# A feed-forward stage with Strassen-like weight blocks: one product moved, unit slots that may wrap, norm sums moved to VectorE, four down-projection chunks

## The reference

```python
x = x + jnp.einsum('btd,de->bte', mix, w_o[l])
h = rmsnorm(x, ln2[l])
gate, up = jnp.split(jnp.einsum('btd,df->btf', h, w_gu[l]), 2, axis=-1)
x = x + jnp.einsum('btf,fd->btd', jax.nn.silu(gate) * up, w_down[l])
```

## Time and profile before

| what | value |
|---|---|
| median of 3 runs (lowest to highest) | 1065.31 us (1064.7 to 1066.32) |
| the profiled execution: its own time, and its span | 1065.55 us, 1063.7 us |
| busy: PE (matmul), DVE, ACT, POOL | 97%, 64%, 47%, 32% |
| share of PE in the chain that ended last | 75% |
| mean granted TensorE clock | 0.995 |

### The profile page before, as it was taken

How to read it: one execution, slowest core, us unless ns; L and a number is a source line. 1 busy time by engine, 2 the same in 40 slices (tenths; PEclk the granted TensorE clock), 3 DMA queues, 4 the chain that set the end, 5 groups by cost and what they waited for, 6 DMA issues and landing times.

```text
span 1063.7 us, 15328 instructions
## 1 busy us (share of the span) xinstructions
PE 1026.7 (97%) x5694; PEld 851.0 (80%) x5694; DVE 682.8 (64%) x1267; ACT 503.3 (47%) x927; POOL 344.0 (32%) x405
## 2 busy tenths in 40 slices
PE   9999999999889999999998999999999999999997
PEld 7887877787679898888887877866787777788886
DVE  6865666477746667666676666799865766425544
ACT  6433566463434344434434645555754554423323
POOL 1354533343221010000100836533435756521101
PEclk9999999999899999999999999999999999999999
DMA  8312332222254454444433846311222333222312
GB/s 288 100 61 80 101 97 75 71 82 77 79 143 114 100 120 95 127 102 114 113 77 89 203 120 199 110 60 59 80 70 83 104 112 109 80 99 80 113 64 79
DMA packets 42681, 109.83 MB, mean 103 GB/s; under 512 B 5472, under 2 KB 8992, under 8 KB 42608
## 3 DMA queue, kind: packets, MB, share of 16 engines
q1 hardware_dynamic: 36720, 96.80, 28.5%
q0 software_dynamic: 5472, 11.54, 6.8%
q10 hardware_dynamic: 416, 0.52, 0.2%
HBM read 100.74 MB, written 4.74 MB: 99 GB/s over the span
## 4 chain that ended last, share of the span: by engine, by line
PE 75%; DVE 15%; ACT 5%; issue 4%; POOL 1%; DVEq 0%; ACTq 0%; POOLq 0%
PE bank L1739 16%; PE bank L1741 16%; PE bank L1740 16%; PE bank L1753 4%; PE bank L1755 4%; PE bank L1754 4%; PE bank L1903 2%; PE bank L1894 2%; DVE score L2573 1%; PE bank L1787 1%; PE bank L1789 1%; PE bank L1788 1%; ACT WH L1956 1%; DVE WL L2211 1%; DVE m L2571 1%
## 5 line engine op out<-in xcount | busy, mean ns | idle before, releaser
L2665 POOL TENSOR_TENSOR WL<-WS,WH 128x256 fp32r<-128x256 f32 x256 | 203.4, 794 | 251.3 <-ACT WH L1956 235.3
L1739 PE MATMUL bank<-HH,WH 128*128 128x512 f32 x600 | 245.4, 409 | 7.2 <-DVE fg L2504 3.0
L1741 PE MATMUL bank<-HH,WL 128*128 128x512 f32 x600 | 235.7, 393 | 0.0
L1740 PE MATMUL bank<-HL,WH 128*128 128x512 f32 x600 | 235.6, 393 | 0.0
L1739 PEld LDWEIGHTS bank<-HH,WH 128*128 128x128 f32 x600 | 113.8, 190 | 35.8 <-issue 3.8
L1956 ACT ACTIVATE WH<-WS 128x1024 fp32r<-128x1024 f32 x128 | 133.0, 1047 | 3.9 <-DMA WS<-wall 2.9
L1741 PEld LDWEIGHTS bank<-HH,WL 128*128 128x128 f32 x600 | 113.4, 189 | 24.8
L1740 PEld LDWEIGHTS bank<-HL,WH 128*128 128x128 f32 x600 | 113.9, 190 | 21.1 <-issue 1.2
L2098 ACT ACTIVATE WH<-SS 128x512 fp32r<-128x512 f32 x112 | 66.5, 622 | 111.5 <-DVE SS L2439 80.4
L2442 DVE TENSOR_TENSOR WL<-SS,WH 128x512 fp32r<-128x512 f32 x112 | 75.7, 689 | 62.4 <-ACT WH L2098 62.4
L2707 POOL DMA_DIRECT2D SS<-wall x32 | 27.8, 870 | 232.4 <-DVE SS L2439 159.3
(11 more groups left out here) (375 smaller groups left out, 2284.8 us busy)
## 6 DMA issues: line engine op xcount, KB each, us to landing
WS<-wall SPq DMA_DIRECT2D x129, 512.0 KB, 3.4
SS<-wall SPq DMA_DIRECT2D x48, 256.0 KB, 3.4
SS<-wall POOLq DMA_DIRECT2D x32, 256.0 KB, 4.0
WL<-wall POOLq DMA_DIRECT2D x6, 512.0 KB, 7.1
scratch<-rows SPq DMA_DIRECT2D x8, 320.0 KB, 4.9
b_t<-scratch SPq DMA_DIRECT2D x8, 256.0 KB, 3.2
X<-xT SPq DMA_DIRECT2D x7, 256.0 KB, 6.5
outT<-X SPq DMA_DIRECT2D x7, 256.0 KB, 2.5
```

Of the source, the lines that this page charges most:

```text
L1739: e.matmul(b[:, :], wh, xh, start=k == 0, stop=False)
L1740: e.matmul(b[:, :], wh, xl, start=False, stop=False)
L1741: m = e.matmul(b[:, :], wl, xh, start=False, stop=k == n - 1)
L2665: e.tensor_tensor(unit_span(WL, u)[:, cs], WS[:, u % NST, cs], f32(unit_span(WH, u)[:, cs]), ALU.subtract).then_inc(*tick(w_low_g, u if c ...
```

## The change

Five edits, all in the feed-forward stage:

- T4 of the group before is issued after T1 instead of before it (`group_at` positions (1,2) to (1,7) become (1,3) to (1,8), T1 goes from (0,3) to (0,2)); the making of B21 goes one position earlier and that of B22 one later, and `line_up` follows.
- `slot` no longer skips: a unit may start in the last slot and wrap, and is then copied and subtracted in two halves (`unit_parts`).
- s3 and s4 are computed on DVE, and the 19 steps are issued at three of five pieces of the plain pairs 1 to 5 rather than at each of the first 19; the loads and blocks of the first group are issued by a table (`FRONT`).
- `CHUNKS` (0, 6, 10, 14, 16, 22) becomes (0, 6, 10, 16, 22): 8 fewer `add_x`. In the last two chunks the first two output tiles are taken alternately.
- At the end, two down pieces are issued before the last T3, and one unit's preparation is moved earlier.

```diff
-CHUNKS = (0, 6, 10, 14, 16, 22)
+CHUNKS = (0, 6, 10, 16, 22)
+LATE = 14
...
         def slot(n, user):
 
-            if slots["next"] % (2 * NW) + n > 2 * NW:
-                slots["next"] += 1
...
-            for name in ("A11", "s1", "A22", "s2", "s4", "A12", "s3"):
+            for name in ("A11", "s4", "s1", "s2", "A12", "s3", "A22"):
...
             elif x == (-1, 2):
+                do("b_load", g=g, name="B21")
+            elif x == (-1, 3):
                 make(g, "B22")
-            elif x == (-1, 3):
-                do("b_load", g=g, name="B21")
...
-            elif x == (0, 3):
+            elif x == (0, 2):
                 make(g, "B21")
                 seven(g, "T1", "s1", o["z"][:, 256:512], True)
...
-            elif x == (1, 2):
+            elif x == (1, 3):
                 seven(g, "T4", "A22", o["z"][:, 256:512], False, corner((g, "C22")))
-            elif x == (1, 3):
+            elif x == (1, 4):
                 corner_of(g, "C21", o["z"], c_u2)
                 s_ring.give(o["zi"], corner((g, "C21")))
                 do("seven_tanh", g=g)
...
+            gens = [product(("down", m, c), "w_down", CHUNKS[c], cols(128 * m), f"gu{c}", n,
+                            down_rest(m) if c == 3 else add_x(("down", m, c), m)) for m in range(8)]
+            if c > 1:
+                for _ in range(n // 2):
+                    yield next(gens[0])
+                    yield next(gens[1])
+            yield from chain(*gens)
...
+        FRONT = {12: (-2, 6), 11: (-1, 0), 9: (-1, 3), 8: (-1, 2), 6: (-1, 4), 2: (-1, 8), 0: (-1, 6)}
...
-                    if left == 7:
-                        group_at(OLD_PAIRS, -2, 6)
-                    if left < 7:
-                        step(OLD_PAIRS - 1, 6 - left)
-                    if j:
+                    if left in FRONT:
+                        group_at(OLD_PAIRS, *FRONT[left])
+                    n_side += j > 0
+                    if j and n_side * 3 % 5 < 3:
                         next(nh, None)
...
-                if at == 2 and (g in unit_of or g == NPAIR - 1):
+                if at == 2 or at == 4 and g == NPAIR - 1:
                     split()
...
+        next(downs)
+        next(downs)
         group_at(last, 1, 0)
         next(downs)
         group_at(last, 1, 1)
-        group_at(last, 1, 2)
+        group_at(last, 1, 3)
         next(downs)
-        group_at(last, 1, 3)
         group_at(last, 1, 4)
-        next(downs)
...
+        def unit_parts(u):
+
+            at_s = unit_at[u]
+            if at_s + 2 <= 2 * NW:
+                return [(slice(0, 1024), slice(512 * at_s, 512 * at_s + 1024))]
+            return [(slice(0, 512), slice(512 * at_s, 512 * at_s + 512)), (slice(512, 1024), slice(0, 512))]
```

More of the change, by code:

```diff
@@ L463, in chunk_of @@
         def chunk_of(j):
-            c = max(c for c in range(5) if CHUNKS[c] <= j)
+            c = max(c for c in range(4) if CHUNKS[c] <= j)
             return f"gu{c}", j - CHUNKS[c]
@@ L1044, in out @@
             def out(b):
-                do("add_x", name=("down", m, 4), m=m, b=b)
+                do("add_x", name=("down", m, 3), m=m, b=b)
                 i, sq, free = sq_ring.take()
@@ L1057, in down @@
             n = CHUNKS[c + 1] - CHUNKS[c]
-            for m in range(8):
-                yield from product(("down", m, c), "w_down", CHUNKS[c], cols(128 * m), f"gu{c}", n,
-                                   down_rest(m) if c == 4 else add_x(("down", m, c), m))
+            gens = [product(("down", m, c), "w_down", CHUNKS[c], cols(128 * m), f"gu{c}", n,
[5 more added lines that the diff above has]
+            yield from chain(*gens)
         assert count["tile"] % UT == 0
@@ L1067, in build @@
         for g in range(OLD_PAIRS, NPAIR + 1):
-            for of, name in ((g - 1, "T3"), (g, "B22"), (g - 1, "T4"), (g, "T1"), (g, "T2"), (g, "B21"), (g + 1, "B11")):
+            for of, name in ((g - 1, "T3"), (g, "B22"), (g, "T1"), (g - 1, "T4"), (g, "T2"), (g, "B21"), (g + 1, "B11")):
+                if g == NPAIR and name == "T3":
+                    line_up.append(("unit", at_unit + len(WITH_UNIT)))
                 if OLD_PAIRS <= of < NPAIR:
                     line_up.append((of, name))
-                if g == NPAIR and name == "T3":
-                    line_up.append(("unit", at_unit + len(WITH_UNIT)))
             if g in unit_of:
                 line_up.append(("unit", unit_of[g]))
-        left = 8 * OLD_PAIRS
+        left, n_side = 8 * OLD_PAIRS, -1
+        FRONT = {12: (-2, 6), 11: (-1, 0), 9: (-1, 3), 8: (-1, 2), 6: (-1, 4), 2: (-1, 8), 0: (-1, 6)}
         for j in range(OLD_PAIRS):
@@ L1098, in build @@
         now["low"] = w_low_v
-        group_at(OLD_PAIRS, -1, 8)
-        downs = chain(*(down(c) for c in range(5)))
+        group_at(OLD_PAIRS + 1, -2, 6)
+        downs = chain(*(down(c) for c in range(4)))
         for g in range(OLD_PAIRS, NPAIR):
             for at in range(7):
-                if at == 2 and (g in unit_of or g == NPAIR - 1):
+                if at == 2 or at == 4 and g == NPAIR - 1:
                     split()
@@ L2209, in vector_program @@
                     elif unit_low[u] is w_low_v:
-                        q.wait_ge(w_hi(u))
-                        e.tensor_tensor(unit_span(WL, u), WS[:, u % NST, :], f32(unit_span(WH, u)),
-                                        ALU.subtract).then_inc(*w_low_v.tick(u))
+                        for cs, at_c in unit_parts(u):
+                            q.wait_ge(w_hi((u, cs.start)))
+                            e.tensor_tensor(WLS[:, at_c], WS[:, u % NST, cs], f32(WHS[:, at_c]),
+                                            ALU.subtract).then_inc(*w_low_v.tick((u, cs.start), *([u] if cs.stop == 1024 else [])))
                 elif kind == "split_first":
@@ L2707, in gpsimd_program @@
                     e.dma_start(SS[:, i, :], wall_block(g, "B12"), accum_op=ALU.add).then_inc(*block_sum[i].tick((g, name)))
-                elif kind == "norm2" and s["what"] in ("s3", "s4"):
-                    what = s["what"]
-                    for c in range(4):
-                        o, p, r = (NF[:, NF_at[n] + 256 * c:NF_at[n] + 256 * c + 256]
-                                   for n in (what, *{"s3": ("A22", "A21"), "s4": ("A12", "s2")}[what]))
-                        q.wait_ge(before[0], norm2_v(("n", 7)) if what == "s3" else norm2_v("s2"))
-                        e.tensor_tensor(o, p, r, ALU.subtract if what == "s3" else ALU.add).then_inc(
-                            *tick(norm2_g, what if c == 3 else (what, c)))
                 elif kind == "ffn_up":
```

78 lines of the change are left out of this document (42 added, 36 removed).

## The result

The changed kernel takes 1047.31 us (median of 4 runs, 1046.58 to 1048.98) against 1065.74 for the one before on the same chip: ratio 0.983 [0.9813, 0.9847]. It is faster, by 18.4 us where 27.5 were forecast. That is 5.8 us above the forecast's own range (1034.5 to 1041.5) and 0.3 above the range over all cases (1034 to 1047). The profiled execution has a span of 1046.0 us; TensorE (PE) is still busy 97% of it, DVE 65%, ACT 48%, POOL 32%.

What follows compares the result with a forecast made beforehand. PE, busy nearly throughout, bounds the kernel, with 35.7 us of waits to gain at most. Gains of 5.1 + 1.1 + 16.8 + 4.5 = 27.5 us gave 1038 us; own range 1034.5 to 1041.5, over all cases 1034 to 1047.

Steps and rivals of the forecast that it cites:

- Plain pairs: Stretch ahead of the first group: DVE sums and the spread steps cut PE's loss from 10.0 to 4.9, gain 5.1 us.
- The 0.5 per instruction: Plain pairs: DVE's low part was longer by 0.5 us beside POOL's sums, read from the earlier trace.
- First period: First group's period: T1's wait goes, T2's low part stays late; lost 2.5 instead of 3.6, gain 1.1 us.
- The ideal of 14.0: First group's period without waits: 7 products and 24 matmuls, 14.0 us of the 17.59 measured before.
- Middle: Fourteen middle periods: T4 later, B11 ahead of the tanh and wrapping units cut the loss from 17.3 to about 0.5, gain 16.8.
- 7.7, 4.3 and 3.5: Middle periods' waits: C22 in ten periods 7.7 us, B11's low part in twelve 4.3, two irregular periods 3.5 with restarts.
- one wait for a bank: Middle periods: with small gaps, the remaining some 1.5 us of loss; the dropped two-k-tile chunk's bank was waited for once.
- The end: Last group's period: waits for the last T3's low part and last C22 nearly go; lost 0.3 instead of 4.8, gain 4.5.
- C22 then ends about 14.25 us into the period: Last group's period: C22 would be ready at about 14.25 us, where T4 is due at 14.16.
- what PE gains ahead of it should be carried to the end: Behind 578.57, the last chunk to the end: same engine order but for a few instructions, so a change of 0 us.
- the end keeps its waits: Rival, last period: one `add_x` or unit ahead of the last C22; 1041 to 1042 us, chance 0.05.
- The rivals at 0.14, 0.09, 0.02 and 0.03: In order: front gives nothing back, 1043; new wait each middle period, 1046 to 1054; late T1 DMA, slower; swallowed later, 1065.

Runs made afterwards that it cites:

- experiment 17: Changed kernel with the block of the first group's T2 made before VectorE reads plain pair 5's up bank: 1047.05 us, 0.9824 to before.
- 8 to 14: Seven runs on the changed kernel undoing T4's place, B11's place, the slot edit and B21's place (last with the gate's step), singly or together: 1045.78 to 1061.01 us.
- Experiment 2: Changed kernel with the weight unit prepared ahead of the last C22 (unit A) prepared behind it: 1044.43 us, 0.9808 to before.
- Experiments 1 and 5: Changed kernel, last chunk's first accumulating-DMA unit (B): low part on VectorE, 1042.13 us; or still by DMA but prepared ahead of the gate's chain, 1042.03 us.
- 4: Kernel before the change, with the low part of the same unit B on VectorE: 1064.6 us, 0.9997 to before.
- both repairs: Changed kernel with unit B's low part on VectorE and unit A prepared behind the last C22: 1040.25 us, 0.9764 to before.
- b21_back: Changed kernel with block B21 made behind B22 again: 1046.99 us, 0.9832 to before.
- t2_early: Changed kernel with the first group's T2 block made before the read of plain pair 5's up bank: 1047.05 us, 0.9824 to before.
- both_ends: Changed kernel with both edits at the stage's end, unit B's low part on VectorE and unit A behind the last C22: 1040.25 us, 0.9764 to before.
- before_u18_on_dve: Apparently the kernel before the change with unit B's low part on VectorE: 1064.6 us, 0.9997 to before.
- u18_early: Apparently the changed kernel with unit B still by DMA but prepared behind the last group's tanh, ahead of its gate chain: 1042.03 us, 0.9786 to before.
- final_best: Not defined by name; apparently the changed kernel with both end repairs plus T2's block made early: 1040.07 us, 0.976 to before.
- u18_on_dve: Apparently the changed kernel with unit B's low part on VectorE instead of by accumulating DMA: 1042.13 us, 0.9782 to before.

## Why the prediction was off

- **Plain pairs** (5.1 forecast, 6.4 found). Right, waits and all: 3.5 us in two waits at pair 4 were forecast, 1.33 and 1.73 came, and the clock stayed at 1.00, where I had allowed for one drop in part. The seven low parts of `halves_normed` took 1.22 to 1.23 us, so POOL lengthened none of them. The 0.5 per instruction was read beside POOL sums of 256 columns, of which the one that fell into a pause of DVE took 0.74; so it is no measure of what a multiplication of 1.29 would cost, and no low part here ran beside one.
- **First period** (1.1 forecast, 0.4 found). The ideal of 14.0 is right for the six products that lie in it; the text says seven. The wait at T2 was forecast at 1.5 to 2 and is 2.2. DVE's part of pair 5 is the reason, as given; that it can't be removed by moving the block ahead of it, since `c_p` then comes as late, is what experiment 17 adds.
- **Middle** (16.8 forecast, 17.2 found). The total was right because it was made of the distance to a bound, PE's own pace, and the change reached the bound. The split was wrong: I gave 7.7, 4.3 and 3.5 to T4, B11 and the skip. Undone alone they are worth 6.1, 0.9 and 0.0; undone one on top of the other 6.1, 0.2 and 2.35, and B21's place with the gate's step, to which I had given nothing, 6.3 (8 to 14). The 7.7 counted ten waits for C22, of which T4's place gives back seven; the other three, 2.0 us, went with the `add_x` of the chunks, whose effect in the middle I had put at one wait for a bank.
- **The end** (4.5 forecast, 0.7 found). This step failed: "C22 then ends about 14.25 us into the period". It ended at 16.6. Unit A's copy waits in ACT's queue for the gate of group 20, and I had followed the two engines one by one. Experiment 2 moves that one unit: C22 then ends at 15.1, and the period is 3.0 us shorter, 1.5 of it clock. So A is 1.5 us of the 2.35 by which C22 was late; the other 0.9 were already there ahead of A, with the gate's chain of group 20 and an `add_x`, and no run takes them apart.
- **Behind it** (0 forecast, +6.2 found). This step failed worst: "what PE gains ahead of it should be carried to the end". The order was the same, but the margins were not read. Unit B had 0.3 us. Moving two down pieces from behind T4 to ahead of T3 takes 2.7 us of PE work from behind T4, so that PE reaches unit B earlier against the gate's chain, in whose queue B's copy stands. Experiments 1 and 5 remove the wait in two ways, and 4 shows that there was none before. Half of the 5.0 us is the longer landing, whose cause stays open. With both repairs the stretch behind the last period is still 1.9 us longer than before (487.0 against 485.1), which is open too.
- **The chances.** The rival "the end keeps its waits" came true (0.05), and together with a wait that stood on no list it went past the range. The rivals at 0.14, 0.09, 0.02 and 0.03 did not happen. None of the three signs that were to show the prediction wrong came either: all three stood in the stretches that went right, and none behind the last period.

## What to carry to other kernels

When an edit pulls work forward on the bounding engine, look at the next transfers behind the seam: read issue, landing and due time of each in the trace of before, take the difference for the margin, and follow the queue of every engine that a transfer's preparation passes. It may be 0.3 us, of which no view of waits says a word. And when a total comes out right, undo the parts in pairs as well as singly before crediting any of them; where two edits free the same chain, taking out either costs nothing.

## What the runs showed of the hardware

The same wait of 2.31 us ahead of the last T4 was followed by the lower clock level in some versions and not in others. Windows of 5 us that begin 2.2 us before the wait ends, first of the changed kernel, then of b21_back (columns as in the earlier trace rows):

```profile
548.00:553.00 5.00, 2.81 (x13) 2.81 (x14) 2.14 (x3) 0.00 (x0) 0.00 (x0) 0.73 0.30 108
```

```profile
547.04:552.04 5.00, 2.75 (x18) 2.53 (x19) 2.20 (x3) 0.01 (x1) 0.00 (x0) 1.00 0.35 108
```

That is 21.1 against 19.6 us for the last period. Of the twelve profiles with this wait at 2.31 (the changed kernel and eleven others), seven show the one and five the other, and none of the edits in them touches the stretch from the last T3 to the end of the wait. In the changed kernel the waits of 1.3, 1.7 and 2.2 us in the first two stretches were not followed by the lower level; the one of 4.8 was, with 0.66 on average from 570 to 575. At T2 of the first group waits of 2.0 to 2.3 us were followed by a mean clock of 0.90 or 0.91 over the period in six profiles, t2_early and both_ends among them, and waits of 1.4 to 2.8 by 1.00 in the others with this spread. So a gap of about 2 us is worth itself or 1 to 1.5 us more, a forecast can't tell which, and a difference of 1 us between two versions may be no more than that.

The first accumulating DMA of 512 KB took 5.6 us from issue to landing before and 8.1 after, with much the same traffic: the windows 583.57 to 589.50 before and 562.40 to 570.40 after have DMA shares of 0.89 and 0.92. What made the difference was not tried. The profiles point at the next such DMA and leave it open: in twelve of them it is issued 2.0 us behind the first one, which took 7.5 to 8.3; in `before`, before_u18_on_dve and u18_early 3.8 to 4.0 us behind, and the first took 5.6 to 5.7. But in both_ends, final_best and u18_on_dve it is issued 6.5 us behind, and the first still took 7.2, 7.5 and 8.0.
